# Hybrid decoder step: expert outputs added into the residual by DMA and a one-hot product, S5 regrouping and taps on two queues

## The reference

```python
for l in range(DEPTH):
    h = _rmsnorm(x, w['norm_mix'][l])
    ...
    x = x + mix.astype(x.dtype)
    x = x + _hmoe(_rmsnorm(x, w['norm_ffn'][l]), ...)
...
# _hmoe: top-1 of 4 groups, top-2 of 8 experts inside it
combine = jnp.sum(jax.nn.one_hot(eid, MOE_EXPERTS) * top_w[..., None], axis=1)
for g in range(MOE_GROUPS):
    act = (silu(x @ w_gate) * (x @ w_up)) * combine[:, sl, None]
    y = y + einsum('nef,efd->nd', act, w_down)
```

## Time and profile before

| | |
|---|---|
| runs | 1294.62, 1296.03, 1293.2 us |
| profiled execution, its own time | 1291.57 us |
| its span, first to last instruction | 1289.8 us |
| mean granted TensorE clock | 0.871 of full speed |
| busy: PE, DVE, ACT, POOL | 924.0 (72%), 378.0 (29%), 183.5 (14%), 365.6 (28%) us |
| chain that ended last, by what it consists of | PE 41%, DMA 35%, DVE 10%, POOL 5%, issue 4% |
| moved by DMA | 289.92 MB, mean 225 GB/s |

### The profile page before, as it was taken

How to read it: one execution, slowest core, us unless ns; L and a number is a source line. 1 busy time by engine, 2 the same in 40 slices (tenths; PEclk the granted TensorE clock), 3 DMA queues, 4 the chain that set the end, 5 groups by cost and what they waited for, 6 DMA issues and landing times.

```text
span 1289.8 us, 15582 instructions
## 1 busy us (share of the span) xinstructions
PE 924.0 (72%) x5582; PEld 569.9 (44%) x5582; DVE 378.0 (29%) x720; ACT 183.5 (14%) x330; POOL 365.6 (28%) x554
## 2 busy tenths in 40 slices
PE   4999988991588888888035077999827777777740
PEld 2888776451444444444035055444425443344320
DVE  3300353626311111112548910020271111111115
ACT  3210201213110111110110004001230101110102
POOL 0060000776466776671580000000032111101011
PEclk9999898995599999999566578999957999999985
DMA  6111315405399999998471935000064999999963
GB/s 219 64 68 66 105 51 206 148 1 213 112 425 421 422 422 418 410 421 344 150 101 14 101 54 233 0 1 1 1 262 182 426 425 423 426 422 421 422 241 150
DMA packets 57387, 289.92 MB, mean 225 GB/s; under 512 B 11971, under 2 KB 21955, under 8 KB 38631
## 3 DMA queue, kind: packets, MB, share of 16 engines
q1 hardware_dynamic: 38359, 251.13, 52.1%
q10 hardware_dynamic: 11424, 21.05, 4.4%
q0 software_dynamic: 7552, 17.06, 3.7%
HBM read 268.39 MB, written 27.13 MB: 229 GB/s over the span
## 4 chain that ended last, share of the span: by engine, by line
PE 41%; DMA 35%; DVE 10%; POOL 5%; issue 4%; SPq 2%; ACT 2%; POOLq 0%; DVEq 0%; ACTq 0%
DMA arena<-in_w_gu 29%; PE ps L590 11%; PE ps L765 11%; PE ps L870 9%; DVE arena L1153 4%; POOL arena L1606 4%; SPq L394 2%; DMA arena<-scratch_kp 2%; PE ps L846 2%; PE ps L850 2%; DVE arena L908 2%; DVE arena L1467 1%; DMA arena<-arena 1%; PE ps L555 1%; DMA arena<-scratch_yd,idx_back 1%
## 5 line engine op out<-in xcount | busy, mean ns | idle before, releaser
L765 PE MATMUL ps<-arena 128*64 128x256 f32 x2048 | 253.5, 403 | 92.6 <-DMA arena<-in_w_gu 92.6
L765 PEld LDWEIGHTS ps<-arena 128*64 128x64 f32 x2048 | 153.2, 144 | 195.1 <-issue 123.9
L1683 POOL TENSOR_TENSOR arena<-arena 128x256 f32<-128x256 f32 (+3 forms) x192 | 132.4, 689 | 43.0 <-POOL arena L1683 40.3
L590 PE MATMUL ps<-arena 128*128 128x260 f32 x640 | 142.1, 382 | 0.0
L755 PE MATMUL ps<-arena 128*64 128x512 f32 x512 | 124.1, 601 | 9.6 <-issue 9.6
L590 PEld LDWEIGHTS ps<-arena 128*128 128x128 f32 x640 | 120.8, 190 | 19.8 <-issue 0.4
L1606 POOL TENSOR_TENSOR arena<-arena 128x32 f32<-128x32 f32 (+4 forms) x159 | 72.6, 456 | 158.5 <-ACTq L1028 143.5
L1450 DVE TENSOR_TENSOR arena<-arena,ps 128x128 f32<-128x128 f32 x64 | 18.5, 289 | 337.5 <-ACT arena L1083 330.0
L870 PE MATMUL ps<-arena 128*128 128x512 f32 x256 | 112.5, 599 | 4.4 <-ACT arena L1124 4.4
L1153 DVE TENSOR_TENSOR arena<-arena 128x160 f32<-128x160 f32 (+14 forms) x144 | 96.3, 669 | 22.1 <-PE ps L578 7.3
L1665 POOL TENSOR_TENSOR arena<-arena 128x1024 f32<-128x1024 f32 x10 | 19.8, 2017 | 270.2 <-ACT arena L1052 270.2
(11 more groups left out here) (199 smaller groups left out, 815.2 us busy)
## 6 DMA issues: line engine op xcount, KB each, us to landing
arena<-in_w_gu SPq DMA_DIRECT2D x64, 2048.0 KB, 13.0
arena<-in_w_down SPq DMA_DIRECT2D x64, 1024.0 KB, 13.5
scratch_yd<-arena ACTq DMA_DIRECT2D x128, 128.0 KB, 9.3
arena<-in_w_in SPq DMA_DIRECT2D x10, 1024.0 KB, 4.9
arena<-in_w_out SPq DMA_DIRECT2D x1, 4096.0 KB, 13.1
scratch_hd<-arena ACTq DMA_DIRECT2D x8, 512.0 KB
arena<-scratch_kp SPq DMA_DIRECT2D x8, 512.0 KB, 20.9
arena<-in_w_glu SPq DMA_DIRECT2D x2, 2048.0 KB, 7.4
```

The source lines that it names most:

```text
L590: mm = pe.matmul(o[:, b, 0:HALF], w[:, kc, (n % 2) * P:(n % 2 + 1) * P], HT[:, kc, b * HALF:(b + 1) * HALF], start=kc == 0, stop=kc == KC - 1)
L765: mm = pe.matmul(ps[CAP * f:CAP * f + CAP, 2 + s, 0:256], XT[s][:, kc % 4, CAP * (kc // 4):CAP * (kc // 4) + CAP], WGU[s][:, kc, 256 * f:2 ...
L1683: g_.tensor_tensor(o, x, y, f).then_inc(sem("matrix_steps"), 1)
```

## The change

1. **Weights.** Each expert's output is multiplied by its tokens' weights as it leaves PSUM (YE = PSUM x WL). WL comes from a second list product on PE, of `ohw` (the one-hots times the weights).
2. **Gathers that add.** The ten gathers go straight to X with `compute_op=ALU.add`, first the five of choice 0, then the five of choice 1, each of which waits for the tile's first. Indices outside the first 30 experts are skipped by the bounds check. They wait for the stores of all pairs but the last.
3. **The last pair.** Its outputs aren't stored: both experts' down products go into one pair of banks (`down_last`), DVE and ACT each scale one half (YL), and PE multiplies it by PICK, the transposed one-hot of which token sits in which of the 128 rows. DVE adds the product to X, a tile at a time, and ACT squares each tile as it is done. The one-hots are made on DVE and transposed on PE behind the lists, ahead of the first token transposes.
4. **Registers.** All engines load `most` ahead of the round, not behind it; SP's first weight loads come after that.
5. **S5 start.** XK's unused rows are filled with zeros by two DMAs, issued when the last down product of layer 0 is done; both BD are made by ACT; all six steps of the phases are made by POOL; regrouping DMAs 0 and 2 are issued by SP, 1 and 3 by ACT; taps 0 to 3 by SP, 4 to 7 by ACT.
6. **The end.** Three tiles of the last norm are scaled by DVE, two by ACT and POOL.
7. Smaller: `keep`, a constant of 512 columns, is made on chip (`KEEP`) and a constant of 128 columns comes in; some semaphores are merged.

The diff, cut to its core:

```diff
@@ PE, turns
-                    for q in range(10):
-                        mm = pe.matmul(ps[:, 0, 0:E], OHR[:, q], oh[q // 5][:, q % 5], start=q == 0, stop=q == 9)
-                    mm.then_inc(sem(f"list_done_{l}"), 1)
-                    pe.wait_ge(sem(f"list_read_{l}"), r + 1)
+                    for b, what in enumerate((oh, ohw)):
+                        for q in range(10):
+                            mm = pe.matmul(ps[:, b, 0:E], OHR[:, q], what[q // 5][:, q % 5], start=q == 0, stop=q == 9)
+                        mm.then_inc(sem(f"list_done_{l}"), 1)
+                    pe.wait_ge(sem(f"lists_{l}"), 3 * r + 3)
+                        pe.wait_ge(sem("picks_made"), l + 1)
+                        for t in range(5):
+                            mm = pe.transpose(pick_slot(t), OHT[:, t], ident)
+                        mm.then_inc(sem("picks_by_pe"), 1)
...
+                    if isinstance(r, int):
+                        pe.wait_ge(sem(f"y_ready_{l}"), E + 2)
+                        pe.wait_ge(sem("picks_by_act"), 2 * l + 2)
+                        for t in range(5):
+                            if t == 3 and l == 0:
+                                pe.wait_ge(sem("m_copied"), 17)
+                            if t == 4:
+                                pe.wait_ge(sem(f"combined_{l}"), 1)
+                            m = ROWS[t]
+                            for b in range(2):
+                                mm = pe.matmul(last_slot(t)[0:m, b, :], PICK[:, t, 0:m], YL[:, b], start=True, stop=True)
+                            mm.then_inc(sem("picks_by_pe"), 1)
@@ DVE, turns
+                    if isinstance(r, int):
+                        for t in range(5):
+                            step(v.tensor_scalar(OHT[:, t], const("last"), CC[:, 0, t:t + 1], None, ALU.is_equal))
+                            stt(OHT[:, t], const("last"), CC[:, 1, t:t + 1], OHT[:, t], ALU.is_equal, ALU.add)
...
-                                v.tensor_copy(YE[2 * half + s], ps[:, 6 + s, :]).then_inc(sem(f"y_ready_{l}"), 1)
+                                w = WL[:, bass.ds(2 * p + s, 1)].broadcast_to((P, 512))
+                                v.tensor_tensor(YE[2 * half + s], ps[:, 6 + s, :], w, ALU.mult
+                                                ).then_inc(sem(f"y_ready_{l}"), 1)
...
-                        v.scalar_tensor_tensor(X[0:m, i, :], YG[0:m, q], pwr[0:m, j, i:i + 1], X[0:m, i, :],
-                                               ALU.mult, ALU.add).then_inc(sem(f"combined_{l}"), 1)
+                            dve.wait_ge(sem("picks_by_pe"), 6 * l + t + 2)
+                            dve.wait_ge(sem(f"yg_in_{l}_{t}"), 32)
+                            v.tensor_tensor(X[0:m, t, :], X[0:m, t, :],
+                                            last_slot(t).rearrange("p b n -> p (b n)")[0:m], ALU.add
+                                            ).then_inc(sem(f"combined_{l}"), 1)
@@ POOL, turns
-                        pool.wait_ge(sem(f"y_out_{l}_{s}"), 256 * r + 288)
+                        pool.wait_ge(sem(f"y_out_{l}_{s}"),
+                                     256 * r + 288 if s < 2 or not isinstance(r, int) else 256)
...
+                    for j in range(2):
+                        for t in range(5):
+                            if j:
+                                pool.wait_ge(sem(f"yg_in_{l}_{t}"), 32 * r + 16)
+                            g_.indirect_dma_start(out=X[0:m, t], out_offset=None,
+                                                  in_=yd_rows[0:stored],
...
+                                                  bounds_check=stored - 1, oob_is_err=False, compute_op=ALU.add
+                                                  ).then_inc(sem(f"yg_in_{l}_{t}"), 16)
@@ ACT, experts
+                step(a.activation(warm, ident[:, 0:1], ACT.Sqrt))
+                junk = place(A, D)
+                for t in range(5):
+                    act.wait_ge(sem(f"combined_{l}"), t + 1)
+                    tile_squares(act, 2 * l + 2, t, junk)
...
@@ ACT, S5
+            for q in range(2):
+                make_bd(q)
+                act.wait_ge(sem("h_2"), 2 * q + 2)
+                regroup(act, 2 * q + 1)
+            act.wait_ge(sem("xk_in"), 128)
             ring.wait_full(act, "k")
             recut(act, step, a.copy, 1)
+            act.wait_ge(sem("taps_out"), 16)
+            ring.wait_full(act, "zs", 7)
+            for s in range(L // 2, L):
+                taps(act, s)
@@ SP, S5
+            sp.wait_ge(sem("down_done_0"), E)
+            load(XK[0:NS, 0:L - 1].rearrange("p l d -> p (l d)"), zr[0:NS], "xk_in")
+            load(XK[NS + NCH:UC, 1:L].rearrange("p l d -> p (l d)"), zr[NS:2 * NS], "xk_in")
...
+            for i in range(0, TILES, 2):
                 sp.wait_ge(sem("h_2"), i + 1)
+                regroup(sp, i)
...
-            for s in range(L):
-                load(TT[CW * s:CW * s + CW], kg[:, :, KZERO - CW * s:KZERO - CW * s + P], "taps_in")
+            for s in range(L // 2):
+                taps(sp, s)
@@ DVE, S5
-            step(v.memset(XK[:, 0:L // 2], 0.0))
-            make_bd(dve, step, v, 1)
...
-            phases(tt, NCH // 2)
@@ POOL, S5
-            pool.wait_ge(sem("x_moe"), 1)
-            step(g_.memset(XK[:, L // 2:L], 0.0))
-            make_bd(pool, step, g_, 0)
+            pool.wait_ge(sem("picks_by_pe"), 6)
...
-            for k in range(5):
+            for k in range(6):
                 phases(tt, 2 ** k)
```

314 lines of the change are left out of this document (199 added, 115 removed).

## The result

Median of 4 runs: **1278.32 us** after (1278.08 to 1278.94), 1294.45 before beside it; ratio 0.9884, 95% interval [0.9863, 0.9905]. I had forecast faster, and 1254 in a range of 1242 to 1273: the direction held, but of the 41 us of gain that I had forecast 16 came.

The account below looks back on a forecast made before the run. It took the expert stages' start times and the serial work behind them to bound the kernel. Starts +6.0, rotation -16.8, taps -15.3, second stage's end -14.2 and constants -0.5 summed to -40.8: 1254 us, range 1242 to 1273.

Parts of the forecast that it names:

- Final scaling: Last norm: three tiles on DVE and two on ACT and POOL would cost 0, between -1.3 and +1.4 us.
- End of the first stage: Behind the first expert stage: with gathers that add, scaling would start from 640.5, not 647.28, -6.8 us.
- Table "being loaded already": Last norm's root behind the second stage: its table is already loaded; branch, mean, root and reciprocal take 1.8 us.
- End of the second stage: Behind the second expert stage: adding gathers at 2.4 us a tile, scaling from 1266.8, not 1280.96, -14.2 us.
- Rotation: S5 start: rotation of zs would start at 673.2, not 690.04, -16.8 us, the first stage's 6.8 within it.
- path (a): Before the rotation: regroup in about 13 us on two queues, not 21.6, then recut and transposes 10.8, done at 665.6.
- (b): Before the rotation: POOL does all phases from 633.3 in 35 us, sample states 4.8, done at 673.1, so late next.
- Taps: S5 stage: taps on two queues take 21.7 us, not 43.3; DVE is late next, first y product -15.3 us.
- Starts: Ahead of each expert stage: added list products, one-hots and transposes cost +3 us each, +6.0 in all.
- the shared rate: Rival, 25%: two queues share one rate, so taps gain 0 and rotation is -14.4; sum -23.1, 1271.5 us.
- The add is not free: Judges a rival, 14%: the gathers' add costs nothing, issuing at 1.35 us a tile limits; sum -52.7, 1242 us.
- the bound at over 5 us: Rival, 6%: adding gathers become the bound at both ends, slower above 5.0 us a tile; at 5.5, 1304 us.

Follow-up runs that it names:

- The one-edit run: The kernel after with the last norm's five scalings all on DVE, none on ACT and POOL: 1272.53 us, against 1278.3 for the kernel after.
- the run where it waits: The kernel after with POOL waiting for the regroup's last DMA before it starts its phases: 1306.73 us, one run, against 1278.3.

## Why the prediction was wrong

The steps that failed most are the two that were put at nothing: the work between the last gate product of the first stage and scaling (down products and loads of zeros), and what follows the last scaling. The direction and most mechanisms were right; the sum of the savings was not.

- **Final scaling: 0, between -1.3 and +1.4. Measured +6.4, far outside its own bounds.** The blocking, for which I had given the upper bound, came out at it: from the start to the end of the scalings it is 8.0 us for 6.6, +1.4. What failed is that I counted to the last scaling and put everything behind it at nothing. The last store landed another 1.3 us later, and the end of POOL's program, which now follows its last multiplication by 7.0 us, keeps the kernel open for 3.7 more. The one-edit run returns 5.8.
- **End of the first stage, -6.8. Measured +2.6.** Three things by rows: the last pair's down products, put at no more than before, take 3.62 an expert against 1.94, as both products of an expert lie in one column group, and the first gather stands 10.6 us behind the last gate product where I had 7.2 (alternating gave back 1.4 of it); the loads of zeros that I called hidden were beside the gathers, not in a free stretch, and cost 3.4 there; the rest, 1.7 to 2.5, is the add at 2.8 us a tile for my 2.4. "POOL's wait for the last M transposes stays" was true, and I didn't ask whether it had to: without it, 4.1 less.
- **Table "being loaded already". Wrong:** a branch lies between the warming root and the real one, and with it gone the load is gone (1.3 a layer). The squares' own order on ACT I had read, the branch not.
- **End of the second stage, -14.2. Measured -9.2:** the first gather is released 1.7 us behind the last gate product, not just ahead of it (2.3), and ten gathers take 25.4 us, not 22.9. The mechanism, the stores of the last but one pair and then the add's rate, was right.
- **Rotation, -10.0 behind scaling. Measured -6.1:** the premise that two queues which write different partitions run side by side held for the taps and failed for the regroup, whose queues took turns. I had taken 8.6 off path (a) for it, of which 2.4 were to reach the rotation, with POOL late next. Paths (a), the recut, and (b), POOL's sample states, end within 0.6 of each other (688.1 and 687.6). POOL, by the late gathers at work from 645.18 on and not from 633.3, blocked DVE's four recut copies (1.32, 0.90, 1.27 and 1.06 us for 0.69 in the run where it waits), and behind the recut the rotation still waited 2.0 us for PE's first zs products (L887, until 690.03), which stood on none of my three paths.
- **Taps, -15.3. Measured -15.6, right,** with rate (196) and releaser (DVE) as forecast; 12.6 by undoing it.
- **Starts, +3 each. Measured +3.6 and +4.9;** in the second, 2.7 more lie ahead of the list product (1.3 of them where the router's new products and the register load are), 4.0 more between it and the first gate product, and 1.8 are caught up within the stage. The quicker clock that I had hoped for came only with the gate products: the 40 list products took 8.74 us at a granted 0.50 (1.2 GHz), and the gate products behind them 8.14, for 9.01 before.
- **Of the rivals** the shared rate (1271.5) came nearest the time and is wrong for the taps, right for the regroup. That two terms of one sum might fall to different sides of the same question was in no case. The add is not free, nor the bound at over 5 us.

The misses were nearly all of one sign, because I worked out savings to their full and let additions be hidden. My range was made of single misses; it had none for several costs of 3 to 6 us at once.

## What to carry to other kernels

Work that is moved off a busy engine onto POOL should be priced beside DVE, not alone: ACT, POOL and DVE together took 8.0 us (1261.23 to 1269.25) for what DVE alone did in 6.1. And a change at the end of a kernel should be counted to the end of every engine's program: POOL's came 7.0 us behind its last multiplication. "Hidden" is a statement about a resource: zeros into 8 partitions were hidden from every engine and not from the gathers. And in a stage bound by weights, as here, what counts ahead of its end is when a buffer is released; look for waits (a branch behind a warmed table, a wait for transposes ahead of a gather) that the change lets you drop; here these two gave 1.1 and 4.1 us.

## What the runs showed of the hardware that I had not expected

Two hardware queues writing different groups of 16 partitions nearly double the rate for packets of 512 B from DRAM (101 to 196 GB/s), and do nothing for 4 KB or 1 KB packets from SBUF (113 to 118): with 4 KB the queues take turns, a whole DMA at a time, with 1 KB they share the rate. A gather that adds runs at 180 to 193 GB/s against 351 for one that copies, and costs 1.56 instead of 0.99 us to issue. Four down products of 64 rows (eight instructions) that all go to one column group take 3.62 us; eight products that alternate between two groups take 3.65 at a granted clock of 1.00, and 5.35 where it fell to 0.50. POOL's closing instruction ends 7.0 us behind its last multiplication (6.95 or 6.96 in all fifteen traces of kernels that multiply on POOL at the end).
